# RWKV scan: parts 0 and 1 of the right-hand side behind a step's first update, sample operations over two levels, last mask ahead of the receptances

## What is computed

```
def step(S, inp):
    r_t, w_t, k_t, v_t, kk_t, a_t = inp
    sa = jnp.einsum('bhvk,bhk->bhv', S, -kk_t)
    S = (S * w_t[:, :, None, :] + sa[..., None] * (kk_t * a_t)[:, :, None, :]
         + v_t[..., None] * k_t[:, :, None, :])
    return S, jnp.einsum('bhvk,bhk->bhv', S, r_t)
```

## Time and profile before

| | us |
|---|---|
| runs | 3018.93, 3019.54, 3026.66 |
| median | 3019.54 |
| profiled execution | 3016.34 |
| its span | 3014.3 |
| TensorE busy in it | 2876.1 |
| VectorE busy in it | 1528.4 |
| the scan, from the first to the last addition of L2983 | 187.0 |

### The profile page before, as it was taken

One profiled execution on the slowest core, in us unless ns is written; L12 is line 12 of the kernel. 1 busy time (PEld: TensorE's weight loads), 2 busy tenths in 40 slices (PEclk: granted clock), 3 DMA queues, 4 the chain that ended last, 5 costly groups with the idle time before them and its releaser, 6 DMA issues.

```text
span 3014.3 us, 72962 instructions
## 1 busy us (share of the span) xinstructions
PE 2876.1 (95%) x29617; PEld 2733.3 (91%) x29617; DVE 1528.4 (51%) x2080; ACT 1085.0 (36%) x2139; POOL 1321.5 (44%) x959
## 2 busy tenths in 40 slices
PE   6999999998989999999998999999999999899998
PEld 5998999997978877899997899889999899799998
DVE  3435666118357874666603242476650444566612
ACT  4224333225455652433323444343332422433322
POOL 3443444442435554344443273434444344344443
PEclk9999999999999999999999999999999999899999
DMA  7544333544411013333354323533334543133332
GB/s 269 164 151 159 95 92 88 158 128 136 119 44 32 4 37 124 120 89 92 99 159 152 99 64 112 169 123 89 92 116 146 173 120 91 57 92 92 91 91 85
DMA packets 465618, 332.56 MB, mean 110 GB/s; under 512 B 19914, under 2 KB 435608, under 8 KB 465122
## 3 DMA queue, kind: packets, MB, share of 16 engines
q1 hardware_dynamic: 461400, 325.24, 35.1%
q10 hardware_dynamic: 4010, 4.22, 0.6%
HBM read 319.62 MB, written 10.20 MB: 109 GB/s over the span
## 4 chain that ended last, share of the span: by engine, by line
PE 62%; DVE 4%; ACT 2%; issue 1%; DMA 1%; SPq 0%; POOL 0%; ACTq 0%; DVEq 0%
PE banks L1667 33%; PE banks L1675 16%; PE banks L2126 5%; PE banks L2133 1%; PE banks L1628 1%; PE banks L1973 1%; DVE h L2662 1%; PE banks L1690 1%; DVE proj L2606 1%; PE banks L1761 0%; DMA s_state<-in_state_wkv_b_dram 0%; ACT conv L1080 0%; PE banks L2135 0%; ACT uv L1433 0%; DVE proj_b L2606 0%
## 5 line engine op out<-in xcount | busy, mean ns | idle before, releaser
L765 POOL TENSOR_TENSOR w_lo<-w_raw,w_hi 128x1024 fp32r<-128x1024 f32 x395 | 1007.5, 2551 | 1108.1 <-ACT w_hi L981 1088.0
L1667 PE MATMUL banks<-u_hi,w_hi 128*128 128x260 f32 x4064 | 834.5, 287 | 14.2 <-ACT w_hi L981 9.4
L1667 PE MATMUL banks<-u_lo,w_hi 128*128 128x260 f32 x4064 | 825.1, 284 | 0.0
L1667 PEld LDWEIGHTS banks<-u_hi,w_hi 128*128 128x128 f32 x4064 | 627.4, 189 | 27.1 <-issue 15.2
L1667 PEld LDWEIGHTS banks<-u_lo,w_hi 128*128 128x128 f32 x4064 | 629.9, 189 | 1.6
L981 ACT ACTIVATE w_hi<-w_raw 128x1024 fp32r<-128x1024 f32 x402 | 424.5, 1056 | 454.2 <-PE banks L1675 284.4
L1675 PE MATMUL banks<-u_hi,w_lo 128*128 128x260 f32 x4064 | 527.5, 282 | 0.0
L1675 PEld LDWEIGHTS banks<-u_hi,w_lo 128*128 128x128 f32 x4064 | 502.1, 187 | 1.3
L1667 PE MATMUL banks<-hid_hi,w_hi 128*128 128x260 f32 x1664 | 336.3, 283 | 0.0
L1667 PE MATMUL banks<-hid_lo,w_hi 128*128 128x260 f32 x1664 | 335.2, 283 | 0.0
L3113 DVE TENSOR_TENSOR csb<-proj 128x520 f32 (+1 forms) x42 | 30.3, 722 | 470.8 <-ACT proj L1048 470.8
(11 more groups left out here) (463 smaller groups left out, 3898.8 us busy)
## 6 DMA issues: line engine op xcount, KB each, us to landing
w_raw<-in_ffn_w_up_dram SPq DMA_DIRECT2D x176, 512.0 KB, 3.7
ada_raw<-in_ada_w_dram SPq DMA_DIRECT2D x96, 512.0 KB, 4.7
w_raw<-in_ffn_w_down_dram SPq DMA_DIRECT2D x64, 448.0 KB, 3.7
w_raw<-in_sconv_w_in_dram SPq DMA_DIRECT2D x48, 512.0 KB, 5.2
ada_ahead<-in_ada_w_dram SPq DMA_DIRECT2D x36, 512.0 KB, 7.7
ada_ahead_down<-in_ada_w_dram SPq DMA_DIRECT2D x36, 512.0 KB, 6.2
w_raw<-in_ffn_w_down_dram SPq DMA_DIRECT2D x32, 512.0 KB, 4.0
ada_pro<-in_ada_w_dram SPq DMA_DIRECT2D x6, 2048.0 KB, 21.2
```

What stands on the lines that cost most here:

```text
L765: pool.tensor_tensor(w_lo[:, s, :, :], w_raw[:, s, :, :], w_hi[:, s, :, :].bitcast(F32), ALU.subtract).then_inc(lo_done, 1)
L1667: pe.matmul(tile_ps[slot][half][0:width, 0:HALF], w_hi[:, s, k, 0:width], x[:, k0 + k, half * HALF:(half + 1) * HALF], start=start and k = ...
```

## The change

On TensorE the first two parts of the right-hand side, with their wait, move from level 1 to right behind the update products of level 0, ahead of the products of the former solution. On VectorE the nine sample operations of two steps are dealt out anew: two of them now stand at level 0, behind the state update, and one at level 1; one or two remain behind the last addition to the right-hand side (L2983) instead of three or four. The last mask of a step goes ahead of the receptances.

```diff
@@ TensorE, scan_step @@
                         update_products(w, q, 0)
+                        pe.wait_ge(st_updated, w + 1)
+                        right_side(q, (0, 1))
                         if w:
                             outputs_of_solution(w - 1, qn)
                             state_products(qn)
...
                         for lvl in range(1, NLV):
                             first_products(w, q, lvl)
-                            if lvl == 1:
-                                pe.wait_ge(st_updated, w + 1)
-                                right_side(q, (0, 1))
@@ VectorE, scan_step @@
-                        samples = (((0,), (1,), (2, 3)), ((4,), (5, 6), (7, 8)))[q]
+                        samples = (((0, 1), (2,), (3,)), ((4, 5), (6,), (7, 8)))[q]
...
-                            if lvl == 1:
-                                for j in samples[0]:
+                            if lvl < 2:
+                                for j in samples[lvl]:
                                     sample_state(c, j)
...
+                        if one_more:
+                            mask_scores(w + 1, 1 - q, 3)
                         if two_more:
                             dve.wait_ge(y_mm, 2 * w + 1)
                             receptances(c + 1, q)
-                        if one_more:
-                            mask_scores(w + 1, 1 - q, 3)
...
-                        for j in samples[1]:
-                            sample_state(c, j)
                         for j in samples[2]:
                             sample_state(c, j)
```

## The result

| | us |
|---|---|
| changed kernel, median of 16 runs | 3027.14 (3022.51 to 3030.66) |
| kernel before, median of 16 runs on the same chip | 3019.51 (3016.36 to 3026.66) |
| ratio, with its 95% interval | 1.0024 (1.0017 to 1.0031) |
| profiled execution of the changed kernel, and its span | 3028.1, 3026.0 |
| the scan in it, first to last addition of L2982 | 196.6 (before 187.0) |

The changed kernel is slower by 7 us, a difference that can be measured but is inside the 0.3% that the prediction calls no change. The forecast was 3021.5 us, 1.9 us of loss.

A forecast was written before the change was run, and what follows sets the result against it. Bound: a chain of latencies in the RWKV scan's steps. Even steps +0.10, odd +0.22, 2.2 us together, less 0.3 in the last: +1.9 us, 3021.5 us. Range from just below 3013.9 to 3029 us.

The forecast's parts named there:

- The sign: Whole kernel: slightly slower, +1.9 us; chances 0.88 same within about 0.3%, 0.10 slower, 0.02 faster.
- The rival in which VectorE is in time: Level 0: both moved operations end before 1007.5, both gains stand, 5.6 us less, 3013.9 us; chance 0.14.
- The right-hand side, 0 to 0.1 us a step: TensorE, before the products of the solution: the moved matmuls fit its 0.51 us of idle time, costing 0 to 0.1 us.
- The 0.18 us of level 1: Level 1 without the right-hand side: at most 0.18 us a step shorter, only if VectorE's addition is not late.
- Level 1's addition, 0.30 us in even and 0.42 in odd steps: VectorE: two sample operations ahead of this addition make it late by 0.30 us in even steps, 0.42 in odd ones.
- the bound of 0.54: Level 1's addition: upper bound of its lateness, 0.54 us, if operation 4 takes 0.92 us.
- At level 2 nothing more is late: VectorE at level 2: even a sample operation of 0.92 us ends at 1009.68, before 1009.72, so no further delay.
- The mask, 0.20 us: End of each step: with the mask ahead of the receptances the turn of the inverse starts 0.20 us earlier.
- The last step, -0.3 us: Step 15: two operations delay level 1's addition about 1.5 us, a shorter tail gives back; net -0.3 us.
- GpSimd and VectorE block each other, 0.98 us a step: Rival, level 0: ct products cost VectorE 0.88 us; 0.98 us a step, 13.7 us in 14 steps, 3032.9 us; chance 0.11.
- Steps of 12.5 to 12.7 us: Scan in the changed trace: the step length expected if the forecast holds, against 12.47 us before.

The follow-up runs named there:

- e2: The kernel before with only the sample operations dealt out as in the change; ratio to the kernel before 1.0033.
- e7: The changed kernel with a single sample operation at level 0 and one at level 1; ratio to the kernel before 1.0002, median 3022.30 us.
- e4: The kernel before with the right-hand side and the mask moved, sample operations left where they were; ratio to the kernel before 1.0001.
- e3: The kernel before with only the last mask put ahead of the receptances; ratio to the kernel before 1.0003.
- e1: The kernel before with only parts 0 and 1 of the right-hand side moved behind level 0's update products; ratio to the kernel before 1.0008.
- e5: The changed kernel with one tiny GpSimd operation ahead of its g 0 addition at level 3; ratio to the kernel before 1.0012.
- e11: The changed kernel unchanged, run and profiled again on another chip; ratio to the kernel before 1.0031, median 3027.83 us.
- e8: e4 with 16 fewer matmuls in each step, so part of the work is left out; ratio to the kernel before 0.9978, 3013.46 us.

## Why the prediction was right, and where its steps were off

It was right in its sign and in its class, by the mechanism that it named. Its size was about a quarter of the measured one, so that the median falls into the range only by the part that was added for the spread of runs; that is luck.

- **The sign, and why.** Right: chance 0.88 for no change within 0.3%, forecast on the slower side, because two operations with their gaps don't fit before level 1's addition. e2 and e7 show it as the cause. The rival in which VectorE is in time falls. The size is short: +1.9 us forecast, about +7 us measured.
- **The right-hand side, 0 to 0.1 us a step:** right. 1009.01 + 0.28 = 1009.29 against a start at 1009.22, no idle time, and 0.02 us more in A (e4 against e3). The 0.18 us of level 1 are real, and show only where VectorE is in time (e1, e4, e7).
- **Level 1's addition, 0.30 us in even and 0.42 in odd steps:** the term that was mis-sized. C grew by 0.34 us in the better even steps (2.57 less 2.23) and by 0.65 in three of them and 0.69 in five of the seven odd ones (2.92), outside the bound of 0.54. Odd steps 9 and 13 have 2.61 and 2.49 us. To the 0.30 us of the fastest rows an odd step adds 0.09 (the gap before the first operation is 0.24 us, where I took 0.15 from the earlier trace rows), 0.31 (operation 4 takes 0.99 us, where I took 0.68 and 0.92 as the bound) and 0.02 (operation 5, 0.71): 0.72 us. An even one adds the gap alone, 0.38, and 0.69 where operation 0 takes 1.00 us. The row for 0.68 stands beside a ct product that started 0.05 us later. I weighed the rule of who starts first for the second operation alone, though the first one starts with ct. In all C gave +6.4 to 6.7 us where 7 x 0.30 + 7 x 0.42 is 5.0.
- **"At level 2 nothing more is late":** right for the additions (0.37 us of idle time before 1015.57). But level 3's first inverse and the build now start together, which I didn't look for: E +0.24 us in 6 to 12 of the 13 steps with a build, 1.1 to 2.6 us in all. No term had it, and e5 shows its cause. (The kernel before has this tie once, 0.73 us at 998.12.)
- **The mask, 0.20 us:** right. 2.43 to 2.46 us became 2.25 us (A) in undisturbed steps, 0.23 us by e3 and e4, and VectorE was idle 0.50 us before L2982, so it waited for TensorE as said.
- **The last step, -0.3 us:** right at the full clock: +1.4 us in C as against 1.5, and 1.82 us less at the end, by e11. The first profile had the lower clock there, and lost the gain.
- **GpSimd and VectorE block each other, 0.98 us a step:** the mechanism is there, its size isn't. It costs 0.3 us ahead of level 1's addition and 0.24 at the build, in the steps where GpSimd wins the tie, not 0.88.
- **What would show it.** No idle time before the products of the solution, none before the addition, no wait for the mask: as listed. Steps of 12.5 to 12.7 us: wrong, 12.8 and 13.2 us in undisturbed even and odd steps.

The sum of the changed kernel by e11: C +6.4, E +1.1, A -2.5, rest -0.7 us, 4.4 us in 14 steps (the first profile: 7.7 us), and the last step with its end -0.2 (or +1.5 at the lower clock). The measured 7 us lie between this and the first profile's 9.2. Some 3 us may be missing in the profile of e11 because that execution was the shortest of its eight, which I leave open.

## What to carry to other kernels

Idle time in front of an operation is room only for what ends in it: lay the moved operations into it with their gaps, and for each one look at what the engine that shares its port starts in the same tenth of a microsecond. A moved operation also shifts later pairs that used to miss each other, so the whole step has to be gone through for new ties, not only the place of the edit. And where an engine runs through hundreds of small instructions, count them: once the waits are gone, their supply can be the next limit. Here 8% fewer matmuls gave some 7 us against e4 (though e8 leaves out part of the work), and the new order alone gave nothing that shows in the time.

## What the runs showed of the hardware that I had not expected

- A tie of 0.01 to 0.02 us between VectorE and GpSimd decides over 0.3 us: the same build took 0.42 or 0.74 us, from step to step and from execution to execution of the same kernel (0.73 us or more in 12 of 13 steps, then 0.70 or more in 6). A GpSimd operation of 0.19 us that goes first costs the build only 0.06 us (0.48).
- In e4 from 1040 to 1070 us TensorE stood still for 0.2 to 0.8 us at six of seven 16384-byte packets of its instruction queue, and went on 2.3 to 2.5 us after their start, with nothing else on the queues. It was 2.5 us in 8 waits before, 5.4 us in 15 in e4 with its shorter steps, and 1.7 us in 7 with 8% fewer matmuls.
- The granted clock at the end of the scan fell to its lower level in one execution of the changed kernel and stayed at 1.00 in another, with the same waits before it; the two ends differ by 1.5 us.
